# One branch per engine at the end, channel statistics on four column strips, and two steps moved in ScalarE's order

## What is computed

```
z = h @ w_in                                  # q | k | v | ret_gate | conv_glu | gate_A | gate_B
A = (groupnorm(retention(q, k, v)) * silu(ret_gate)) @ w_ret_out
c = depthwise_conv31(glu(conv_glu)) + conv_b
B = silu(layer_norm(c)) @ w_conv_out          # mean and variance of c over its 1024 channels
h = LN1(alpha*h + (sigmoid(gate_A)*A + sigmoid(gate_B)*B) @ w_out)
moe = top-1 of 4 groups, top-2 of 8 SwiGLU experts in the group
pe  = (p @ w_ple_proj) * sigmoid(h @ w_ple_gate)
y = LN2(alpha*h + moe + pe)
```

## Time and profile before

| | |
|---|---|
| median of 3 runs | 926.77 us (925.39 to 926.88) |
| the profiled execution | 927.27 us, span 925.1 us |
| PE, DVE, ACT busy | 860.6, 422.5, 263.5 us |
| mean granted TensorE clock | 0.989 |
| HBM read, written | 258.38 MB, 13.09 MB |

### The profile page before, as it was taken

One profiled execution on the slowest core, in us unless ns is written; L12 is line 12 of the kernel. 1 busy time (PEld: TensorE's weight loads), 2 busy tenths in 40 slices (PEclk: granted clock), 3 DMA queues, 4 the chain that ended last, 5 costly groups with the idle time before them and its releaser, 6 DMA issues.

```text
span 925.1 us, 16495 instructions
## 1 busy us (share of the span) xinstructions
PE 860.6 (93%) x6604; PEld 554.6 (60%) x6604; DVE 422.5 (46%) x781; ACT 263.5 (28%) x362; POOL 49.4 (5%) x89
## 2 busy tenths in 40 slices
PE   8999999999999899899999998989888889898975
PEld 5997777889999796675444444434343434444431
DVE  5588999989967468864311110101010101011035
ACT  5454235454237533433111211112121211111110
POOL 1300000000000000000000000000000000000000
PEclk9999999999999999999999999999999999999997
DMA  8835233143342435737999999999999999999961
GB/s 316 274 143 147 91 137 137 46 139 135 137 151 97 176 137 226 320 137 292 405 421 422 422 422 422 422 423 421 423 421 422 423 422 422 422 423 421 421 240 57
DMA packets 40516, 266.66 MB, mean 288 GB/s; under 512 B 6214, under 2 KB 6486, under 8 KB 9632
## 3 DMA queue, kind: packets, MB, share of 16 engines
q1 hardware_dynamic: 36064, 255.30, 68.9%
q0 software_dynamic: 4416, 10.86, 3.6%
HBM read 258.38 MB, written 13.09 MB: 293 GB/s over the span
## 4 chain that ended last, share of the span: by engine, by line
PE 56%; DMA 32%; DVE 6%; ACT 3%; issue 2%; SPq 1%; DVEq 0%; ACTq 0%
DMA raw_x<-wstream 31%; PE ps L1584 12%; PE ps L1271 7%; PE ps L1273 6%; PE ps L1272 6%; PE ps L1595 3%; PE ps L1555 3%; PE ps L1308 2%; PE ps L1290 2%; PE ps L1310 2%; PE ps L1309 2%; ACT w_hi L472 1%; PE ps L1375 1%; DVE w_lo L722 1%; PE ps L1318 1%
## 5 line engine op out<-in xcount | busy, mean ns | idle before, releaser
L1584 PE MATMUL ps<-raw_x,xs 128*64 128x512 f32 x1024 | 233.6, 596 | 36.2 <-DMA raw_x<-wstream 35.0
L1584 PEld LDWEIGHTS ps<-raw_x,xs 128*64 128x64 f32 x1024 | 79.9, 136 | 161.2 <-issue 159.2
L1595 PE MATMUL ps<-raw_x,actT 128*64 128x512 f32 x512 | 117.8, 597 | 0.0
L722 DVE TENSOR_TENSOR w_lo<-raw_dense,w_hi 128x2048 fp32r<-128x2048 f32 x44 | 101.8, 2313 | 33.1 <-ACT w_hi L472 33.0
L1197 DVE COPY actT<-ps 128x256 f32<-128x256 f32 x32 | 13.6, 424 | 222.7 <-PE ps L1602 222.7
L855 DVE SCALAR_TENSOR_TENSOR cT_sb<-uT_sb,conv_par,cT_sb 128x350 f32<-128x350 f32 x210 | 106.5, 573 | 0.6
L472 ACT ACTIVATE w_hi<-raw_dense 128x2048 fp32r<-128x2048 f32 x44 | 84.0, 1908 | 79.6 <-PE ps L1290 44.6
L1271 PE MATMUL ps<-hT_hi,w_hi 128*128 128x320 f32 x304 | 95.5, 314 | 0.2 <-issue 0.2
L1273 PE MATMUL ps<-hT_hi,w_lo 128*128 128x320 f32 x304 | 93.9, 309 | 0.0
L1272 PE MATMUL ps<-hT_lo,w_hi 128*128 128x320 f32 x304 | 93.9, 309 | 0.0
L1203 DVE SCALAR_TENSOR_TENSOR act_rows<-gate_silu,slot_weight,ps 64x512 f32<-64x512 f32 x32 | 23.7, 740 | 140.2 <-ACT gate_silu L661 140.2
(11 more groups left out here) (290 smaller groups left out, 1055.2 us busy)
## 6 DMA issues: line engine op xcount, KB each, us to landing
raw_x<-wstream SPq DMA_DIRECT2D x192, 1024.0 KB, 24.2
raw_dense<-wstream SPq DMA_DIRECT2D x45, 1024.0 KB, 4.9
y_rows<-rows_sb POOLq DMA_DIRECT2D x10, 256.0 KB, 8.8
ln_gb<-ln POOLq DMA_DIRECT2D x2, 1024.0 KB, 5.6
y_gathered<-y_rows SPq DMA_DIRECT2D x4, 512.0 KB, 5.0
const<-consts SPq DMA_DIRECT2D x1, 1294.5 KB, 12.3
rows_sb<-x SPq DMA_DIRECT2D x2, 512.0 KB, 3.7
ln_gb<-ln_in POOLq DMA_DIRECT2D x1, 1024.0 KB, 5.0
```

Of the source, the lines that this page charges most:

```text
L722: tt(wlo[:, i % 2, :], raw_d[:, i % RAW_D, :], whi[:, i % 2, :].bitcast(F), ALU.subtract).then_inc(ss("lo_ready"), 1)
L1584: m = mm(ps[rows_at, 1, :], xs[:, 4 * half + k, :], w[i][:, k, :], start=half == 0 and k == 0, stop=half == 1 and k == 3)
L1595: m = mm(ps[64 * b:64 * b + 64, 4, :], aT[:, 2 * half + k, :], w[:, k, FF * b:FF * b + FF], start=half == 0 and k == 0, stop=half == 1 and ...
```

## The change

Four edits. The constant block gets 32 columns of 1/32 (`C_PART`). The two channel sums are made in two stages: eight products of 32 output columns each, tile `j` on column strip `j % 4` (`part_sums`), a copy of the four strips' partial sums to SBUF by DVE (`cparts`), and one product with `meanw` (`whole_sums`), which is put into the middle of the next `wide`, behind its first nine products (`within`). In ACT's order `hi(30)` now stands ahead of the squares, `hi(32)` ahead of all eight SiLUs, and the sigmoid of chunk 30 ahead of `hi(32)` instead of behind the SiLUs. On PE the branch on the flag now stands ahead of the last expert's down products: both sides of it have their own copy of the end (`finish`, `sums`), the side that is run starts two of the six sums of `y_last` ahead of the down products in place of the warming products, and adds `base_rows` last. On SP two branches on the flag become one.

```diff
-    CT_PARTS = (range(2), range(2, KT), ())
+    CT_PARTS = ((), range(KT), ())
...
-        SIGMOIDS_AT = {c + 1: (c,) for c in [*range(GA0, RET0), GB0, GB0 + 1]}
-        SIGMOIDS_AT[GB0 + 5] = (GB0 + 2, GB0 + 3)
+        SIGMOIDS_AT = {c + 1: (c,) for c in [*range(GA0, RET0), GB0, GB0 + 1, GB0 + 2]}
+        SIGMOIDS_AT[GB0 + 5] = (GB0 + 3,)
...
-            if i == 29:
+            if i == 30:
                 act.wait_ge(ss("conv_out1"), 32)
                 for j in range(KT):
                     act.wait_ge(ss("centred"), j + 1)
                     go(sq[:, j, :], cT[:, j, :], ACT.Square).then_inc(ss("squared"), 1)
...
+                dve.wait_ge(ss("mean_parts"), 1)
+                dve.wait_ge(ss("states_out"), 16)
+                V.tensor_copy(cparts[:], ps[:, 7, 0:CCOLS]).then_inc(ss("mean_parts_in"), 1)
                 dve.wait_ge(ss("mean_ready"), 1)
...
+                dve.wait_ge(ss("var_parts"), 1)
+                V.tensor_copy(cparts[:], ps[:, 7, 0:CCOLS]).then_inc(ss("var_parts_in"), 1)
...
-                m = mm(ps[:, 7, 0:CCOLS], meanw, cT[:, j, :], start=j == 0, stop=j == KT - 1)
+                m = part_sums(j, cT)
             return m
+
+        def part_sums(j, src):
+
+            c = j % 4
+            return mm(ps[32 * c:32 * c + 32, 7, 0:CCOLS], const[:, C_PART:C_N], src[:, j, :], start=j < 4, stop=j >= 4)
+
+        def whole_sums(parts_in, signal):
+
+            pe.wait_ge(ss(parts_in), 1)
+            mm(ps[:, 7, 0:CCOLS], meanw, cparts[:], start=True, stop=True).then_inc(ss(signal), 1)
...
-        mean(range(5, KT)).then_inc(ss("mean_ready"), 1)
-        wide(GB0 + 1, 1, hT, TOK, 22)
+        mean(range(5, KT)).then_inc(ss("mean_parts"), 1)
+        wide(GB0 + 1, 1, hT, TOK, 22, within=lambda: whole_sums("mean_parts_in", "mean_ready"))
...
+        def finish(r, keep=False):
             pe.wait_ge(ss("act_ready"), r * EXPERTS + EXPERTS)
-            keep_warm(1, bank=6)
+            if not isinstance(r, int):
+                keep_warm(1, bank=6)
             act_transposes()
-            keep_warm(WARM[9], bank=6)
+            if keep:
+                pe.wait_ge(ss("back_T"), 1)
+                pe.wait_ge(ss("y_ready"), EXPERTS - 1)
+                from_kept(0, 0, start=True)
+                from_kept(2, 0, start=True)
+            else:
+                keep_warm(2, bank=6)
             pe.wait_ge(ss("aT_ready"), r * EXPERTS + EXPERTS)
             pe.wait_ge(ss("y_ready"), r * EXPERTS + EXPERTS - 1)
             down(r, PAIRS - 1, 10)
...
         with pe.If(flag > 0):
+            finish(0)
             with pe.Fori(1, ROUNDS) as r:
                 rounds(r)
...
+                finish(r)
+            sums(False)
+        with pe.Else():
+            finish(0, keep=True)
+            sums(True)
```

More of the change, by code:

```diff
@@ L52 @@
 C_P = C_FOLD + 36
-C_N = C_P + 1
+C_PART = C_P + 1
+C_N = C_PART + 32
 NOWHERE = 4096
@@ L91, in _constants @@
     c[:, C_P] = p
+    c[:, C_PART:C_N] = 1.0 / 32
     return c.astype(np.float32)
@@ L198, in _program @@
     cstat = a.put("cstat", [128, CCOLS], F)
+    cparts = a.put("cparts", [128, CCOLS], F)
     at_tmp = Area(nc, spot["ret"] + 4096, 3584).put("at_tmp", [128, 2, TOK], F)
@@ L385, in _ @@
         flag = sp.value_load(more[0:1, 0:1], min_val=0, max_val=1)
[L386 to L389, removed]
         def load_rows(stored):
@@ L397, in _ @@
         with sp.If(flag > 0):
+            with sp.Fori(1, ROUNDS) as r:
+                refill(r, 0)
+                refill_from(r)
             load_rows(ROUNDS * EXPERTS - LAST)
@@ L619, in _ @@
                     go(sq[:, j, :], cT[:, j, :], ACT.Square).then_inc(ss("squared"), 1)
-                act.wait_ge(ss("route_in"), 32)
-                go(w_route_r[:, :, 0, :], w_route[:], ACT.Copy).then_inc(ss("route_hi"), 1)
             if i == 30:
@@ L624, in _ @@
                 go(pT[0][:], pT_raw[:], ACT.Copy).then_inc(ss("pT_hi_s"), 1)
+                act.wait_ge(ss("route_in"), 32)
+                go(w_route_r[:, :, 0, :], w_route[:], ACT.Copy).then_inc(ss("route_hi"), 1)
             if i == 33:
@@ L1273, in three, with wide @@
             return mm(out, wl, xh, start=False, stop=last)
-        def wide(c, par, src, cols, credit, banks=None):
+        def wide(c, par, src, cols, credit, banks=None, within=None):
             pe.wait_ge(ss("lo_ready"), c)
@@ L1284, in wide @@
                               src[0][:, k, :], src[1][:, k, :], k == 0, k == KT - 1)
+                    if within and t == 0 and k == 2:
+                        within()
             m.then_inc(ss("pe_done"), 1)
@@ L1475, in _ @@
             pe.wait_ge(ss("squared"), j + 1)
-            m = mm(ps[:, 7, 0:CCOLS], meanw, sq[:, j, :], start=j == 0, stop=j == KT - 1)
-        m.then_inc(ss("var_ready"), 1)
-        wide(GB0 + 2, 0, hT, TOK, 23)
+            m = part_sums(j, sq)
+        m.then_inc(ss("var_parts"), 1)
+        wide(GB0 + 2, 0, hT, TOK, 23, within=lambda: whole_sums("var_parts_in", "var_ready"))
         wide(GB0 + 3, 1, hT, TOK, 24)
@@ L1654, in rounds, with from_kept, from_base, sums @@
             down(r, PAIRS - 1, 10)
+        def from_kept(t, l, start=False):
+            q = ROWS[t]
+            for c in range(2):
+                mm(sum_psum(t)[:, 512 * c:512 * c + 512], backT[64 * c:64 * c + 64, l, 128 * t:128 * t + q],
+                   y_last[64 * c:64 * c + 64, l, :], start=start, stop=False)
+        def from_base(t):
+            q = ROWS[t]
+            pe.wait_ge(ss("base_sum"), t + 1)
+            for c in range(2):
+                m = mm(sum_psum(t)[:, 512 * c:512 * c + 512], ident[:, 0:q], base_rows[:, t, 512 * c:512 * c + 512], start=False, stop=True)
+            m.then_inc(ss("sum_psum"), 1)
+        def sums(kept):
+            pe.wait_ge(ss("back_T"), 1)
+            pe.wait_ge(ss("y_ready"), EXPERTS)
+            for t in range(TILES):
+                if t == 1 or not kept:
+                    from_kept(t, 0, start=True)
+                from_kept(t, 1)
+                from_base(t)
         rounds(0)
```

7 lines of the change are left out of this document (3 added, 4 removed).

## The result

The changed kernel takes 920.06 us (median of 6 runs, 918.10 to 922.89), the kernel before beside it 926.08 us (6 runs). The ratio is 0.9945, interval 0.9929 to 0.9961: 5.1 us less. The profiled execution took 921.15 us, its span 919.0, against 927.27 and 925.1 before.

What follows compares the result with a forecast made beforehand. The experts' weight stream at the memory's rate was taken as the bound, with serial chains before and after it. 927.27 - 2.0 (statistics) - 4.0 (end) = 921.3, 920.8 against the median, stated as 921.0; range 919.2 to 924.3.

Steps and rivals of the forecast that it cites:

- The end: From the last weights to DVE's second tile: moving the jump gains 4.0 us, between 0.2 and 5.3.
- by the same run-ahead: PE's end: flag loaded as the down products ahead of it begin, at 884.6, jump starting at 885.4.
- the jump's length: PE's branch at its new place: 5.5 us instead of 7.08, lower end 0.05, since the queues are half empty.
- DVE's own bound: At the end: DVE free at 902.81, second tile at 904.7 at the earliest, bounding the gain at 5.3 us.
- The clock's charge: PE's end after 2.7 us idle: 1.2 us charged for the lower clock, at the worst 3.4 us.
- The statistics: Mean and variance stage up to the convolution: strips and ACT's order gain 2.0 us, between 0.7 and 2.4.
- The rival with the clock: Statistics stage: the clock falls while PE waits for squares; the end alone counts, 922 to 923; within a rival of chance 0.10.
- The edits costed at nothing: `hi(30)` moved early in ACT's order and SP's single branch at the end: each worth nothing.
- The jump of 7.1 us at the new place: Rival at PE's end: jump stays 7.08 us and the clock falls, 922.5 to 924.6 us; chance 0.22.
- the packet wait behind the last weights: Rival at PE's jump: instruction packet queues behind the experts' last weights, slower or level; chance 0.08.
- The statistics give nothing: Rival: strips give nothing or pairs only, or the clock falls; end alone counts, 922 to 923; chance 0.10.
- The full stream: Experts' weight DMAs: microseconds saved before the first expert start the stream that much earlier, one for one.

Runs made afterwards that it cites:

- the second series: The changed kernel measured again, unedited, against the kernel before on another chip: ratio 0.9957, 4.0 us less.
- the two halves apart: Kernel before with PE's and SP's end edits alone: ratio 0.9966, -3.1 us; changed kernel with the old end (statistics alone): 0.9995, -0.5 us.
- the near side: PE's branch sides exchanged so the side that is run isn't jumped to: in the kernel before ratio 0.9947, in the changed kernel 0.9938.
- kept warm: Statistics edits alone plus five unread 256-column products on PE behind the projection, against the kernel before: ratio 0.9970, -2.8 us.
- the first series: First measurement of the changed kernel beside the kernel before: ratio 0.9945, 920.06 us for 926.08.
- the old end: PE's and SP's end as in the kernel before; with it, statistics alone 0.9995, strips alone 0.9991, ACT's order alone 1.0009.

## Why the prediction was right, and where its terms were not

It said 921.0 us; 920.06 was measured, and 920.96 in the second series, both in the range. That it came so close is in part luck. 6.0 us were costed, 5.1 and 4.0 measured, and the two halves apart gave 3.6, nearly all of it from the end. The kernel before ran at 926.08 and 925.37 us in these series instead of 926.77, which hides a part of the lack.

**The end: 4.0 us costed, 3.1 measured alone, 3.8 in the trace after.** The mechanism was right: the jump keeps its packet, less stands behind it, and DVE nearly binds. Two numbers in it erred and cancelled. The jump was to start 3.35 us ahead of the rows' issue (885.4 for 888.75) and started 1.56 ahead (884.92 for 886.48). The first is the flag's load "by the same run-ahead": it was to come as the down products ahead of it begin, as in the earlier trace rows, and came 1.7 us after that (884.05 for 882.32). What held the sequencer is the landing of the weights for the second half of these products. The first weight load behind that wait, in the changed kernel:

```profile
884.03 0.20 PEld L1613 LDWEIGHTS ps<-raw_x,actT 128*64 128x64 f32 x4 [0.68 <-DMA raw_x<-wstream]
```

The flag's load follows it by 0.02 us, here and in the six other kernels with the branch at this place. The kernel before has the same wait at the same products:

```profile
886.30 0.20 PEld L1595 LDWEIGHTS ps<-raw_x,actT 128*64 128x64 f32 x4 [0.67 <-DMA raw_x<-wstream]
```

Read from this line the jump would have been put at 887.19 (0.02 and 0.87 us later), 1.56 us ahead of the rows' issue, as measured. The second is the jump's length, 3.70 us and not 5.5: I took the busy share of the DMA engines as what lengthens it, but a share of 0.50 did not delay the packet, which was late only where the rows' loads stood ahead of it. Late by 1.8 and short by 1.8, PE's idle came out at 2.71 us for 2.7. From PE's resumption to the second tile it was 15.3 us where 15.1 was costed. DVE's own bound moved meanwhile: its additions ended 15.2 us after the rows' issue, where the 902.81 of the kernel before is 14.1. The clock's charge in it, 1.2, was about 1.5: `y_last` products and down products ran at 0.50 from 889.7 to 893.1, and took 3.1 and 4.1 us where the same ones take 2.1 and 3.65 with the near side.

**The statistics: 2.0 us costed, 0.5 measured.** This is the term that failed, and it failed at one inference: "the 2.4 us idle at the projection left the clock at its upper level (2.4 GHz)", taken as good for the idle that moves ahead of the convolution. An idle of 2.2 us there was followed by 3.4 us at 0.50, which cost 1.4 us; kept warm, the same kernel gave 2.8. The rival with the clock had it at the wait for the squares, where it never fell. Besides, the convolution began 1.3 us earlier and not 2.0. `wide(29)` ended 17.2 us after the mean began (276.77 - 259.58), where 16.5 was costed (277.5 - 260.96): 0.25 us of it lies in the strips, 1.30 and 0.72 us for 1.18 and 0.59, the rest in the hand-overs around them. Squares and variance took 4.6 us for 4.75, `wide(30)` 7.9 for 7.6, and from there to the convolution it was 16.9 for 17.0.

**The edits costed at nothing.** `hi(30)` was said to be worth nothing, since `lo(30)` was done before it was needed. With strips and the squares ahead of `hi(30)`, PE waits 1.3 us for `lo(30)`; so the strips had used up that cover, and the step was wrong, though in the changed kernel the squares' move hides it. SP's single branch was not tried by itself.

**The rivals.** The jump of 7.1 us at the new place did not happen, nor did the packet wait behind the last weights: it moved 1.0 us after the jump's start. "The statistics give nothing", held at 0.10, did in the main, by the clock at a place that it did not name. Its 922 to 923 us are what the ratio of the second series makes of the 926.77 us that the prediction started from (922.8); the first series makes 921.7 of it. The whole exceeds its halves by 0.4 and 1.5 us, and the intervals hold both.

**The full stream.** That microseconds ahead of the first expert carry through is borne out: from the start of the convolution's second chunk to the first expert it is 108.7 to 108.9 us in all thirteen executions.

## What to carry to other kernels

Put the side of a branch that is nearly always run where it follows the branch without a jump, before moving work around the branch: in this kernel that alone gave at least as much as the whole rewriting. A microsecond saved on one engine that leaves TensorE idle ahead of a long chunk may be given back by its clock; look at the granted clock behind each new idle stretch, not only at the idle, and try filling it with products that nobody reads. When one producer gets faster, look again at the order of the other engine that feeds the same stage, and test each of its moves beside the new producer, since here two of them, tried together, paid beside it and the third cost.

## What the runs showed of the hardware

- A taken jump on PE's sequencer to code that isn't fetched took 3.36 to 3.84 us where its packet moved 1.0 us after it, and 6.96 to 7.30 us where transfers of rows stood ahead of the packet and it moved 4.1 to 4.5 us after. A branch not taken took 0.076 us.
- An instruction packet beside the rows may cost them too: in the five kernels with the far jump ahead of the rows' issue the last row load landed 11.2 to 12.6 us after the first issue, in the three with the near side 10.6 to 10.8. With the old end, where the packet comes later, it was 10.9 to 12.1, so this stays an impression.
- An idle of 2.2 us on PE ahead of the convolution was followed by 3.4 us at clock 0.50 in five of six executions, one of 2.4 to 2.9 us at the moved jump in five of five, and one of 2.4 us at the projection in none of four (clock 1.00 in the earlier trace rows). Around an idle of 3.8 us at the projection the clock was at 0.50 for 6.8 us. The length of the idle alone does not tell whether the clock falls.
- Four 32-column strips of TensorE work side by side on fp32 products of 350 columns: ten passes in 1.37 us by the timeline, where the full-width ones took 3.11.
